# Background products and queries on TensorE in two halves, one behind each row's sum

## The reference

```
q = (x @ w_q) -> 8 heads x 2 halves x 128          # the queries
scores = q . sub_keys                              # 128 keys for each half
16 best of each half -> 256 sums -> the 16 best sums = 16 experts
gates = softmax(of the 16 sums)
h[t,h,k] = u_tab[id[t,h,k]] . x[t]                 # a 1024-wide dot product
act = gates * gelu(h)
out[t] = sum over 8 heads x 16 experts of act * v_tab[id]
```

## Time and profile before

| | us |
|---|---|
| median of 3 runs | 1421.67 |
| lowest and highest | 1417.94, 1422.74 |
| the profiled execution | 1421.98 |
| its span | 1420.3 |
| PE, DVE, ACT, POOL busy in the span | 1130.9, 1078.1, 938.8, 625.0 |
| bytes moved in the span | 581.98 MB, mean 410 GB/s |

### The profile page before, as it was taken

The page is one execution under the profiler, slowest core; times in us unless marked ns, Lnnn a source line. Parts: engine busy times, 40 slices in busy tenths (PEclk is TensorE's granted clock), DMA queues, the critical chain, the costliest instruction groups (busy, mean ns, idle before and its releaser), DMA issues.

```text
span 1420.3 us, 19525 instructions
## 1 busy us (share of the span) xinstructions
PE 1130.9 (80%) x6884; PEld 890.8 (63%) x6884; DVE 1078.1 (76%) x2602; ACT 938.8 (66%) x1617; POOL 625.0 (44%) x572
## 2 busy tenths in 40 slices
PE   9999999998789877696756987877667866776566
PEld 4567777676677776666656566765555655555455
DVE  1488877778778887678766668988887788878857
ACT  2245778679877988766645666667666766667563
POOL 1044444344444554444433434444444555444451
PEclk9999999999889999998777988898789988888968
DMA  9899999999999999999999999999999999999994
GB/s 351 311 383 409 422 425 425 426 425 425 402 426 419 424 423 425 425 424 417 431 422 425 426 426 406 426 425 426 426 426 413 404 423 426 426 425 426 425 400 170
DMA packets 94476, 581.98 MB, mean 410 GB/s; under 512 B 10237, under 2 KB 15781, under 8 KB 31914
## 3 DMA queue, kind: packets, MB, share of 16 engines
q0 software_dynamic: 79552, 536.91, 90.5%
q1 hardware_dynamic: 14826, 43.83, 8.0%
HBM read 578.60 MB, written 2.10 MB: 409 GB/s over the span
## 4 chain that ended last, share of the span: by engine, by line
DMA 40%; PE 30%; DVE 15%; ACT 8%; issue 6%; POOL 2%; SPq 0%; DVEq 0%; POOLq 0%; ACTq 0%
DMA arena<-in_uv,ids 39%; PE ps L1269 11%; DVE arena L1914 8%; ACT arena L1536 3%; PE ps L1082 3%; PE ps L948 3%; POOL arena L691 2%; PE ps L1159 2%; PE ps L740 2%; ACT actv L1529 1%; PE ps L757 1%; PE ps L896 1%; PE ps L824 1%; PE ps L821 1%; ACT L1576 1%
## 5 line engine op out<-in xcount | busy, mean ns | idle before, releaser
L691 POOL DMA_INDIRECT arena<-in_uv,ids x556 | 619.9, 1115 | 734.5 <-DVE hid L1914 338.0
L1269 PE MATMUL ps<-ident,arena 128*128 128x128 f32 x4076 | 608.9, 308 | 273.0 <-ACT arena L1536 271.2
L1269 PEld LDWEIGHTS ps<-ident,arena 128*128 128x128 f32 x4076 | 533.3, 159 | 364.6 <-ACT arena L1536 321.4
L1914 DVE CUSTOM_DVE_ANT_1 arena<-arena 128x1024 f32<-128x1024 f32 x384 | 467.7, 1224 | 187.2 <-DMA arena<-in_uv,ids 183.8
L1536 ACT ACTIVATE arena<-arena,actv 128x1024 f32<-128x1024 f32 x511 | 554.2, 1131 | 0.3 <-ACT actv L1529 0.2
L1526 ACT ACTIVATE gel<-hid 128x2 f32<-128x2 f32 (+1 forms) x257 | 52.0, 202 | 356.0 <-DVE hid L1914 353.2
L1914 DVE CUSTOM_DVE_ANT_0 arena<-arena 128x1024 f32<-128x1024 f32 x128 | 155.4, 1223 | 61.1 <-DMA arena<-in_uv,ids 58.5
L1529 ACT ACTIVATE actv<-gel,gates 128x1 f32<-128x1 f32 x511 | 122.9, 287 | 8.4
L948 PE MATMUL ps<-arena 128*128 128x128 f32 x992 | 120.3, 281 | 0.0
L948 PEld LDWEIGHTS ps<-arena 128*128 128x128 f32 x992 | 118.2, 199 | 0.0
L1082 PE MATMUL ps<-arena 128*128 128x384 f32 x192 | 65.9, 486 | 0.0
(11 more groups left out here) (269 smaller groups left out, 1018.1 us busy)
## 6 DMA issues: line engine op xcount, KB each, us to landing
arena<-in_wq SPq DMA_DIRECT2D x9, 1024.0 KB, 10.2
arena<-in_uv,ids POOLq DMA_INDIRECT x556, 3.8
arena<-in_w_out SPq DMA_DIRECT2D x2, 2048.0 KB, 11.3
arena<-in_w_gate SPq DMA_DIRECT2D x1, 4096.0 KB, 17.2
arena<-in_w_out SPq DMA_DIRECT2D x3, 1024.0 KB, 13.1
arena<-in_w_k SPq DMA_DIRECT2D x4, 512.0 KB, 7.9
arena<-in_w_q SPq DMA_DIRECT2D x2, 1024.0 KB, 10.2
arena<-in_w_v SPq DMA_DIRECT2D x2, 1024.0 KB, 10.2
```

Source lines behind the costliest of these rows:

```text
L691: nc.gpsimd.indirect_dma_start(out=dst, out_offset=None, in_=a["uv"][:, :], in_offset=bass.IndirectOffsetOnAxis(ap=ids[:, u % 4, c:c + 1], ...
L1269: i = mm(ps[:, run_bank(r) + k // 4, (k % 4) * P:(k % 4 + 1) * P], v_row(u, c)[:, k * P:(k + 1) * P], ident[:, :], is_transpose=True, star ...
L1914: v.tensor_tensor_reduce(out=r, in0=r, in1=x1[t], scale=1.0, scalar=0.0, op0=ALU.mult, op1=ALU.add, accum_out=hid[:, i, c:c + 1]).then_inc ...
```

## The change

On PE a new function `products(step, part)` takes the products out of `background`. Part 0 (the first two of four chunks) runs behind the odd row's sum, ahead of what is left in `background`; part 1 (the other two) runs behind the next even row's sum. The queries are split too: the first eight matmuls behind row 10 or 11 as before (or 6 or 4), the other eight behind the next row. Waits stand at part 0 and signals at part 1. Nothing is computed in another way, no matmul is added or taken away, and the other engines' programs are as they were.

```diff
-            def project_half(bank, src, w, j):
-                for c in range(WB):
+            def project_half(bank, src, w, j, part):
+                for c in range(2 * part, 2 * part + 2):
...
+            def products(step, part):
+
                 for p in range(NP):
                     for half in range(2):
                         if step == HALF_AT[p][half]:
-                            piece_half(p, half)
+                            piece_half(p, half, part)
+                for t in range(1, NT):
+                    for i in range(1, 5):
+                        if step == out_step(t, f"p{i}"):
+                            out_product(t, i, part)
+                for i in range(NT - 1):
+                    b = TAIL_AT[TAILS[i]]
+                    if step == b + 1 and i == 0 and part == 0:
+                        pe.wait_ge(bias_kept, 2)
+                    if step in (b + 1, b + 2):
+                        k = 4 * (step - b - 1) + 2 * part
+                        gate_product(i, 0, HALF, k, k + 2, 6)
+                    if step in (b + GATE_1, b + GATE_1 + 1):
+                        k = 4 * (step - b - GATE_1) + 2 * part
+                        gate_product(i, HALF, D, k, k + 2, 4)
...
                 for c in range(TOPK):
                     combine(u, c)
+                    if c % 2 == 0 and u * TOPK + c:
+                        products((u * TOPK + c) // 2 - 1, 1)
                     if u == 0 and c == 0:
-                        query(1)
+                        query(1, 0)
+                        query(1, 1)
...
-                    if c == query_row(u) and u + 2 < NU and u + 2 not in EARLY:
-                        query(u + 2)
-                    for e in kept_early(u, c):
-                        query(e)
+                    for half in range(2):
+                        if c == query_row(u) + half and u + 2 < NU and u + 2 not in EARLY:
+                            query(u + 2, half)
+                        for e in kept_early(u, c - half):
+                            query(e, half)
                     if c == 12 and u + 2 < NU:
                         key_scores(u + 2)
                     if c % 2:
+                        products(u * NG + c // 2, 0)
                         background(u * NG + c // 2)
```

More of the change, by code:

```diff
@@ L892, in sum_squares @@
                 return i
-            def project_half(bank, src, w, j):
-                for c in range(WB):
+            def project_half(bank, src, w, j, part):
+                for c in range(2 * part, 2 * part + 2):
                     i = mm(ps[:, bank, :], src[:, c, :], w[:, c, j * HALF:(j + 1) * HALF],
-                           start=(c == 0), stop=(c == WB - 1))
+                           start=(c == 0), stop=(c == WB - 1), skip_group_check=True)
                 return i
@@ L933, in x_transposes, with query @@
                 block_transposes(4, x1[t], j).then_inc(x_tr, 1)
-            def query(u):
+            def query(u, half):
                 t, h, b = UNITS[u]
[L937 to L950, removed]
+                if half == 0:
+                    pe.wait_ge(wq_in[b], 16 * len(wq_homes[b]) * wq_load(u)[1])
+                    pe.wait_ge(score_used, EARLY[u][0] + 2 if u in EARLY else u)
+                    if t == 0:
+                        pe.wait_ge(x1T_ready, 2)
+                    else:
+                        wait_taken(piece_of(t, 7))
+                        wait_taken(piece_of(t, 8))
+                    if u > 1:
+                        pe.wait_ge(qs_ready, Q_NO[u] - 1)
+                for k in range(KD):
+                    i = mm(ps[:, 7, half * P:(half + 1) * P], wq[b][k][:, half * P:(half + 1) * P],
+                           x1T[t][:, k, :], start=(k == 0), stop=(k == KD - 1), skip_group_check=True)
+                if half == 1:
+                    i.then_inc(q_done, 1)
             def key_scores(u):
@@ L1096, in out_piece @@
                     sum_squares(bank, gsq[t - 1], 1).then_inc(piece_done, 1)
[L1097 to L1104, removed]
-                        pe.wait_ge(wout_in[0], 16)
-                    project_half(bank, attnT[t], w_outA, i // 2 - 1).then_inc(piece_done, 1)
                 elif i in (5, 6):
@@ L1188, in embedding_product @@
                 m.then_inc(embedding_done, 1)
-            def background(step):
+            def products(step, part):
                 for p in range(NP):
@@ L1193, in background @@
                         if step == HALF_AT[p][half]:
-                            piece_half(p, half)
+                            piece_half(p, half, part)
[13 more added lines that the diff above has]
+                        gate_product(i, HALF, D, k, k + 2, 4)
+            def background(step):
                 for t in range(1, NT):
@@ L1211, in background @@
                         out_piece(t, 0)
-                    for i in range(1, 5):
-                        if step == out_step(t, f"p{i}"):
-                            out_piece(t, i)
                     for j in range(2):
```

35 lines of the change are left out of this document (23 added, 12 removed).

## The result

The changed kernel takes 1426.51 us (median of 22 runs, 1421.87 to 1428.24) against 1421.41 for the kernel before (22 runs beside them): a ratio of 1.0035, 95% interval 1.0027 to 1.0042, or 5.0 us slower. The forecast was no change. The profiled execution took 1425.55 us with a span of 1423.8, 3.5 above the span of before; single executions of one kernel differ by some 3 us either way, so places are read from the traces and sizes from the medians.

The account below looks back on a forecast made before the run. The prediction took transfers at a 426 GB/s ceiling as the bound. All terms were booked at 0, with 0.5 us off for odd gathers going sooner: 1421.98 - 0.5 = 1421.5 us, range 1416.5 to 1426.5.

Parts of the forecast that it names:

- What bounds the kernel: Whole span: transfers, with a ceiling of 426 GB/s; 581.98 MB take 1366 us of the span of 1420.3.
- The rival that took PE's 271.2 us at its word: POOL's waits for PE's sums: PE's share was real, so faster, 1416.9 to 1418, written as 1417.5; chance 0.14.
- Even rows earlier: PE from 160 to 260 us: even rows' sums 1.3 to 1.7 us sooner, held gathers 1 to 2 sooner; worth nothing.
- Odd rows later: Where PE is not full: odd row's sum up to 1.7 us later, 3.4 at the lower clock; booked 0.
- The key scores: 14 units with the query behind row 11: scores 1.8 us later at 414.37, DVE's cover mostly 3.2 and more; booked 0.
- Products ready later: Products for DVE and ACT: about 1 us later with PE full, up to 3 elsewhere, least cover 1.7; booked 0.
- The slower rival: 340 to 600 us: PE falls behind as the clock drops to 0.75; four gaps, about 7 us, 1428.5; chance 0.16.

Follow-up runs that it names:

- products alone: The changed kernel with the queries whole again and the products still in halves: 1424.82 us, ratio 1.0015 to the kernel before.
- unit 8's query alone: The kernel before with only unit 8's query computed in two halves: 1424.08 us, ratio 1.0013.
- units 5 to 11: Queries split only in units 5 to 11, all other queries and all products whole as in the kernel before: 1426.23 us, ratio 1.0036.
- query a row earlier: The kernel before with each query whole but one row earlier, the five early ones unmoved: 1425.80 us, ratio 1.0031.
- control: The kernel before with two table loads added on ACT behind the copy of unit 24's query: 1423.01 us, ratio 1.0007.
- one split product: The kernel before with only step 43's output product in halves: 1423.43 us, ratio 1.0013.
- pieces: The kernel before with only the projection pieces of steps 16 to 35 in halves: 1423.40 us, ratio 1.0016.
- held ACT: The kernel before with two table loads added on ACT behind the copy of unit 8's query: 1425.81 us, ratio 1.0023.

## Why the prediction was wrong, by its own steps

**What bounds the kernel: right.** The bytes and the ceiling of 426 hold, and the loss is in places where the transfers ran dry. POOL's five excess pauses are still there, 98 rows apart, from 355.6 to 1357.0 us. The rival that took PE's 271.2 us at its word is refuted.

**Even rows earlier: right in its worth, wrong in its sign.** The full stage went from 426 to 427. Sums came last there 16 times, not less than 12; with products alone it is 6 times, by 2.2 us. Neither moved the rate.

**Odd rows later: the failed booking.** The prediction found the weak place, rows 144 to 165 with 1.4 us of lead, and then booked 0 since a pause of 3.37 us cost nothing at 170.40. That precedent is from a stage in which PE is full, but ACT and DVE are not. From 470 to 500 POOL has pauses of 3.97, 4.69 and 4.49 us behind late sums, with ACT packed, and the trace loses 3 us there.

**The key scores: the step that failed most.** It priced the later query by DVE's cover for the scores (3.2 us and more) and passed over ACT, whose copy the scores wait for. It wrote the copy's new time down, 1.8 us later, and did not ask what stands behind the copy on ACT: 20 us without idle time. For the query it worked out, at 414.37, the copy came 1.5 us late. At 461.90 it was 1.88, near the 1.8 by chance: 0.9 for the sum between the halves and 1.0 for PE's later arrival. Booked at 0, it cost 1.8 us (0.1 to 3.4) for unit 8's query alone and 5.1 with those of its neighbours.

**Products ready later: wrong once.** Its least cover was 1.7 us and its worst delay 3. Step 43's product had 3.4 us of cover and was 4.7 late in the changed kernel's trace: the sum between, PE's pause for ACT, and 2.98 us for a half that takes 1.88. Where the half took 1.88, DVE waited 0.9 us or less.

**The slower rival** had the right stretch, the right size (1428.5, measured 1426.5) and the right point of decision: gaps of more than 4 us between gathers, here 4.69 and 5.27. Its mechanism was wrong, so it came near by luck: it had four such gaps for about 7 us, and the kernel is 5.0 slower. The clock of 340 to 600 is 0.92, not 0.75; halves were slow only behind single pauses. It was given a chance of 0.16. As for the rule quoted there (the Trainium skill, Perfetto Trace Analysis, Matmul Optimizations, on back-to-back batches): over the stage this trace does not bear it out, 0.91 before and 0.92 after; behind the pause of 4.62 us it does, with 3.16 us in place of 1.88, and behind pauses of 2.3 to 2.6 us only in two traces of six.

What stays open: why the costs do not add (unit 8's query 1.8, all of units 5 to 11 5.1, products 2.1, the whole change 5.0), what products alone lose behind row 150, and why the query a row earlier costs 4.4.

## What to carry to other kernels

When a piece of work is made ready later, price it for every engine that takes it in order, not only for the last reader: list what stands behind the taking instruction up to that engine's next idle time, and that whole row is late by the same amount. A wait that costs nothing in one stage says nothing of another; ask which engines have idle time to make it up there. And a total of waits is no price: with 38.8 us of ACT's waits nothing was lost that the times could show, and one that grew by about 1 us at the wrong place went with a loss of 1.8.

## What was not expected of the hardware

A half product (two chunks, four matmul records of 512 columns) took 1.88 us where PE came to it without a pause. At step 73 PE paused 4.62 us, and all three traces with that half have it slow: 3.16, 3.22 and 3.44 us. At step 43 PE paused 2.30 to 2.57 us, and the half took 1.88 in four traces and 2.98 and 3.15 in two, the slow ones behind 2.30 and 2.43. So after a short pause the same order of work can come out fast or slow. A row's sum of eight behind the pause took 1.97 and 1.72 in the changed kernel in place of 1.04. With the odd row's sum behind a slow half, a pause on PE lengthens itself by 1.1 to 1.6 us. Ratios of about a thousandth were measured for changes whose place no trace shows: 1.0007 for a control, 1.0013 for one split product, and 1.0016 for pieces in a stage that stayed at 426 GB/s. Only the interval of the last leaves out no change. A single variant's 1.5 us should not be read as an effect here. Some of the costs named above (the pieces, step 43, even unit 8's query by its time alone) are of that size; unit 8's stands because the held ACT, the times of units 5 to 11 and the seven traces that lose 1.4 to 3.2 us behind row 150 agree.
